# A hybrid decoder trunk on eight cores: the attention mask moves from a matmul to a minimum on VectorE, and the expert loops get three overflow weight buffers

## The reference, cut to what matters

```
layer 0:  h += ShortConv(RMSNorm(h));            h += MoE(RMSNorm(h))
          k, v = split(RMSNorm(h) @ W_kv), rotary on k
layer 1:  h += SlidingWindowAttention(RMSNorm(h)); h += MoE(RMSNorm(h))
out = RMSNorm(h)

attention: blocks of 128 queries; the keys are those of the block before and of the block itself
  diff = qi - kj + BLOCK
  band = (diff >= 0) & (diff < WINDOW)          # WINDOW = BLOCK = 128
  s = where(valid, s, -1e30);  p = softmax(concat([s, sink]))[..., :-1];  o = p @ v
MoE: 4 groups of 8 experts; every token takes the top 2 experts of its top group
  out += (silu(t @ w_gate[e]) * (t @ w_up[e]) * combine[:, e]) @ w_down[e]
```

## Time and profile before

| | before |
|---|---|
| median of 3 runs | 1888.91 us (1885.78 to 1893.54) |
| the profiled execution | 1888.96 us, span of its slowest core 1887.9 us |
| spans of the 8 cores | 1857.4 to 1887.9 us |
| PE busy | 1374.8 us (73%) |
| DVE, ACT, POOL busy | 784.3, 806.6, 556.0 us |
| the 16 DMA engines | 325.18 MB moved, 172 GB/s on average |
| HBM | 574.05 MB read, 171.44 MB written |

### The profile page before, as it was taken

One profiled execution on the slowest core, in us unless ns is written; L12 is line 12 of the kernel. 1 busy time (PEld: TensorE's weight loads), 2 busy tenths in 40 slices (PEclk: granted clock), 3 DMA queues, 4 the chain that ended last, 5 costly groups with the idle time before them and its releaser, 6 DMA issues.

```text
span 1887.9 us, 34378 instructions; the slowest of 8 cores (1857.4 to 1887.9 us)
## 1 busy us (share of the span) xinstructions
PE 1374.8 (73%) x11371; PEld 969.8 (51%) x11467; DVE 784.3 (42%) x2116; ACT 806.6 (43%) x1592; POOL 556.0 (29%) x596
## 2 busy tenths in 40 slices
PE   3899299953487586773589888889853688788744
PEld 2787277732366465652335444454332566666533
DVE  2667177763122132221334555555452223232267
ACT  2454155431133233332476667566631234343354
POOL 4001111215132232322544333423214333232270
PEclk8999699976788798886788889889875899898965
DMA  9999987953989789687999545753683698889687
GB/s 166 263 222 113 129 116 110 161 112 110 201 208 218 192 212 238 151 216 176 168 144 152 114 86 105 137 90 73 91 156 123 167 263 213 273 225 278 181 282 253
DMA packets 104966, 325.18 MB, mean 172 GB/s; under 512 B 35009, under 2 KB 45633, under 8 KB 95960
## 3 DMA queue, kind: packets, MB, share of 16 engines
q0 software_dynamic: 63968, 191.22, 57.1%
q1 hardware_dynamic: 40824, 131.75, 20.1%
HBM read 574.05 MB, written 171.44 MB: 395 GB/s over the span
## 4 chain that ended last, share of the span: by engine, by line
PE 44%; DMA 30%; DVE 8%; issue 8%; ACT 7%; POOL 2%; DVEq 0%; ACTq 0%; another core or an unknown queue 0%; POOLq 0%; SPq 0%
PE psb L906 10%; DMA sb_wov<-wcat,sb_o_rw 8%; DMA sb_arena<-wcat 7%; PE psb L445 6%; DMA xs<-sb_xr,sb_slot 5%; PE psb L925 5%; DMA sb_arena<-wcat,sb_o_rw 4%; PE psb L1203 4%; PE psb L1260 3%; PE psb L614 3%; DMA sb_arena<-w_in 2%; PE psb L496 2%; PE psb L868 2%; PE psb L1298 2%; PE psb L1263 2%
## 5 line engine op out<-in xcount | busy, mean ns | idle before, releaser
L913 DVE TENSOR_TENSOR sb_hd<-psb,sb_sil 128x256 bf16<-128x256 f32 (+1 forms) x128 | 58.6, 458 | 515.3 <-PE psb L906 481.6
L906 PE MATMUL psb<-sb_xT,sb_arena 128*128 128x160 bf16 x2048 | 185.9, 260 | 77.3 <-DMA sb_arena<-wcat 76.1
L906 PEld LDWEIGHTS psb<-sb_xT,sb_arena 128*128 128x128 bf16 x2048 | 172.7, 110 | 103.9 <-issue 103.0
L445 PE MATMUL psb<-sb_xnA,sb_arena 128*128 128x256 bf16 (+1 forms) x1728 | 199.7, 275 | 16.2 <-DMA sb_arena<-w_in 11.7
L445 PEld LDWEIGHTS psb<-sb_xnA,sb_arena 128*128 128x128 bf16 x1728 | 166.6, 102 | 40.5 <-issue 21.4
L925 PE MATMUL psb<-sb_arena,sb_hd 128*32 128x512 bf16 (+1 forms) x600 | 157.3, 390 | 2.5 <-issue 0.8
L162 POOL DMA_INDIRECT xs<-sb_xr,sb_slot x66 | 68.3, 1035 | 263.2 <-DVE sb_cv L464 108.5
L933 ACT ACTIVATE sb_yh<-psb 32x1024 f32<-32x1024 f32 x64 | 64.8, 1013 | 182.6 <-PE psb L925 182.6
L911 ACT ACTIVATE sb_sil<-psb 128x256 f32<-128x256 f32 (+1 forms) x128 | 52.8, 412 | 209.2 <-PE psb L906 208.5
L875 ACT ACTIVATE sb_xT<-psb 128x1024 bf16<-128x1024 bf16 (+1 forms) x96 | 76.1, 810 | 127.7 <-PE psb L868 76.0
L1287 DVE TENSOR_TENSOR sb_OT<-psb,sb_rden 64x256 bf16<-64x256 f32 x128 | 53.3, 417 | 172.4 <-ACT sb_rden L1284 99.6
(11 more groups left out here) (187 smaller groups left out, 2750.8 us busy)
## 6 DMA issues: line engine op xcount, KB each, us to landing
wst<-wcat POOLq DMA_DIRECT2D x76, 768.0 KB, 18.8
sb_arena<-wst SPq DMA_DIRECT2D x38, 1536.0 KB, 15.4
sb_arena<-wcat POOLq DMA_DIRECT2D x26, 1536.0 KB, 15.1
ys<-sb_ym SPq DMA_DIRECT2D x64, 512.0 KB, 10.5
sb_xg<-xs SPq DMA_DIRECT2D x64, 256.0 KB, 8.2
xs<-sb_zrow POOLq DMA_DIRECT2D x1, 10240.0 KB, 95.7
sb_h<-xT POOLq DMA_DIRECT2D x8, 1024.0 KB, 63.7
ys<-sb_yh SPq DMA_DIRECT2D x64, 128.0 KB, 9.9
```

What stands on the lines that cost most here:

```text
L445: tr.op("pe", lambda e: e.matmul(ph(bank, half, n), lhsT=wcol(j, c, part), rhs=xn[p2][:, c, :n], start=(c == 0), stop=(c == NCH - 1)), rea ...
L906: tr.op("pe", lambda e: e.matmul(ps[:, bank * 512 + f * n:bank * 512 + (f + 1) * n], lhsT=w_[:, col:col + 128], rhs=x_[:, c, 0:n], start=( ...
```

## The change

**Mask.** The mask matmul is gone: the second score matmul closes the bank. After the exponential, DVE takes, in place, the minimum of `PT` and a table that holds 3e38 where a key may be seen and 0 elsewhere. It is one `tensor_tensor` of 128 x 1024 in bf16 for a unit, with the table broadcast over the 4 query heads. It stands in `SC`, behind the exponential.

**Expert loops.** A third buffer for overflow weights; `load_wo` of block j + 3 follows block j. The list `held` is gone: every main expert's load goes out in `DN` of the expert three before. The first overflow step follows main expert 3 and not 2. To make room, `xo` has four buffers for five, `xh` one for two, and the two `yh` tiles lie in one, on partitions 0 to 31 and 32 to 63.

```diff
@@ phase_moe
-                NW, NXO, NXT = 3, 5, 5
+                NW, NXO, NXT, NWO = 3, 4, 5, 3
-                wo1 = sb(st_, "wov", [128, 6144], BF16)
-                wo = [wo1[:, :], arena[:, 3, :]]
+                wo1 = [sb(st_, "wov%d" % i, [128, 6144], BF16) for i in range(2)]
+                wo = [wo1[0][:, :], arena[:, 3, :], wo1[1][:, :]]
-                for i in range(2):
+                for i in range(NWO):
                     tr.op("pool", lambda e: e.memset(wo[i], 0.0), writes=woB[i])
-                    xh = [sb(s2, "xh%d" % i, [128, D], BF16) for i in range(2)]
+                    xh = [sb(s2, "xh", [128, D], BF16)]
-                    yh = [sb(s2, "yh%d" % i, [T2, D], F32) for i in range(2)]
+                    yh_ = sb(s2, "yh", [2 * T2, D], F32)
+                    yh = [yh_[T2 * i:T2 * i + T2, :] for i in range(2)]
@@ the list of steps
-                        want = -(-(e - 1) * J // (NE - 2)) if e > 1 else 0
+                        want = -(-(e - 2) * J // (NE - 3)) if e > 2 else 0
@@ DN
                             if i + NW < NE:
-                                if (i + NW) in STAGED[l]:
-                                    load_w(l, i + NW)
-                                else:
-                                    held.append(i + NW)
+                                load_w(l, i + NW)
                         else:
...
-                            if i + 2 < J:
-                                load_wo(i + 2)
-                            while held:
-                                load_w(l, held.pop(0))
+                            if i + NWO < J:
+                                load_wo(i + NWO)
@@ the loop
-                    for j in range(2):
+                    for j in range(NWO):
                         load_xo(j)
                         load_wo(j)
...
                         DN(k)
-                        if k == 2 or seq[k] == ("m", NE - 1):
-                            while held:
-                                load_w(l, held.pop(0))
@@ SC
-                                                           start=(K_ is KA), stop=False),
-                                  reads=[KB_[r][k_]] + QB_[q][k_], writes=[PB[kbi]], sig=False)
-                        tr.op("pe", lambda e: e.matmul(o, lhsT=identb[:], stop=True, start=False,
-                                                       rhs=mask[:, kbi * 128:kbi * 128 + 128].unsqueeze(1).to_broadcast([128, 4, 128])),
-                              reads=[tabB, cB], writes=[PB[kbi]])
+                                                           start=(K_ is KA), stop=(K_ is KB)),
+                                  reads=[KB_[r][k_]] + QB_[q][k_], writes=[PB[kbi]], sig=(K_ is KB))
                     tr.op("act", lambda e: e.activation(out=PT[ui % 2][:], in_=ps[:, 0:1024], func=AF.Exp, scale=0.125),
                           reads=[PB[0], PB[1]], writes=[PTB[ui % 2]])
+                    pt = PT[ui % 2][:, :].rearrange("p (k i x) -> p k i x", k=2, i=4)
+                    tr.op("dve", lambda e: e.tensor_tensor(out=pt, in0=pt, in1=mask[:, :].rearrange("p (k x) -> p k x", k=2).unsqueeze(2)
+                                                           .to_broadcast([128, 2, 4, 128]), op=ALU.min),
+                          reads=[tabB], writes=[PTB[ui % 2]])
@@ prep_shared
-    S["mask"] = f(np.concatenate([np.where(k > q, 0.0, -30000.0), np.where(k <= q, 0.0, -30000.0)], axis=1))
+    S["mask"] = f(np.concatenate([np.where(k > q, 3e38, 0.0), np.where(k <= q, 3e38, 0.0)], axis=1))
```

More of the change, by code:

```diff
@@ L810, in phase_moe @@
                     xgB = [Buf("xg%d" % i) for i in range(3)]
-                    xh = [sb(s2, "xh%d" % i, [128, D], BF16) for i in range(2)]
-                    xhB = [Buf("xh%d" % i) for i in range(2)]
+                    xh = [sb(s2, "xh", [128, D], BF16)]
+                    xhB = [Buf("xh")]
                     xT = [sb(s2, "xT%d" % i, [128, NCH, CAP], BF16) for i in range(NXT)]
@@ L831, in load_x @@
                         if e % 4 == 0:
-                            g, q = e // 4, (e // 4) % 2
+                            g, q = e // 4, 0
                             tr.dma("sp", "xh%d" % q, [(xh[q][:].bitcast(U16), xs[4096 + g * 128:4096 + (g + 1) * 128, :], xsB, [xhB[q]])])
@@ L840, in load_wo @@
                     def load_wo(j):
-                        p = j % 2
+                        p = j % NWO
                         tr.idma("wo%d" % p, [(wo[p], O["rw"][:, ovcol[j]:ovcol[j] + 1], wcat_d[l][:], False, NE * 128 - 1, [O["B"]], woB[p])])
@@ L860, in of @@
                             return i, CAP, w[i % NW], wB[i % NW], xT[i % NXT], xTB[i % NXT]
-                        return i, 128, wo[i % 2], woB[i % 2], xU[i % 3], xUB[i % 3]
+                        return i, 128, wo[i % NWO], woB[i % NWO], xU[i % 3], xUB[i % 3]
                     def turn(src, sB):
@@ L888, in XT @@
                             g = i // 4
-                            b, pv = turn(xh[g % 2], xhB[g % 2])
+                            b, pv = turn(xh[0], xhB[0])
                             for r in range(4):
@@ L932, in DN @@
                             tr.op("dve", lambda e: e.tensor_copy(out=ym[p][:], in_=y2(4, 128)), reads=[PB[4], PB[5]], writes=[ymB[p]])
-                            tr.op("act", lambda e: e.activation(out=yh[p][:], in_=y2(6, T2), func=AF.Copy),
+                            tr.op("act", lambda e: e.activation(out=yh[p], in_=y2(6, T2), func=AF.Copy),
                                   reads=[PB[6], PB[7]], writes=[yhB[p]])
                             tr.dma("sp", "ym%d" % p, [(ys[i * 128:(i + 1) * 128, :], ym[p][:].bitcast(I32), [ymB[p]], [ynew()])])
-                            tr.dma("sp", "yh%d" % p, [(ys[4096 + i * T2:4096 + (i + 1) * T2, :], yh[p][:].bitcast(I32), [yhB[p]],
+                            tr.dma("sp", "yh%d" % p, [(ys[4096 + i * T2:4096 + (i + 1) * T2, :], yh[p].bitcast(I32), [yhB[p]],
                                                        [ynew()])])
                             if i + NW < NE:
-                                if (i + NW) in STAGED[l]:
-                                    load_w(l, i + NW)
-                                else:
-                                    held.append(i + NW)
+                                load_w(l, i + NW)
                         else:
@@ L958, in phase_moe @@
                     overflow_setup(l, 7)
-                    for j in range(2):
+                    for j in range(NWO):
                         load_xo(j)
                         load_wo(j)
-                    for j in range(2, NXO):
+                    for j in range(NWO, NXO):
                         load_xo(j)
-                    held = []
-                    last_ov = max(j for j in range(J) if j % 2)
+                    last_ov = max(j for j in range(J) if j % NWO == 1)
                     for k in range(K):
```

2 lines of the change are left out of this document (1 added, 1 removed).

## The result

The changed kernel takes 1818.40 us (median of 4 runs, 1814.97 to 1828.48) against 1888.38 for the kernel before in the same session; the ratio is 0.9635, with a 95% interval of 0.9592 to 0.9678. It is 70 us faster, where 99 were forecast.

The account below looks back on a forecast made before the run. It took the expert loops to be set by transfers or their order, the stream stage mostly by PE. Loops 35 + 28, starts 4 + 2 and mask 30 made 99 us: about 1790, range 1750 to 1855 holding 0.8.

Parts of the forecast that it names:

- rival 3: Stream stage: the mask gives nothing, as the minimum is 1.28 us or DVE's order delays rotary products; 1820, chance 0.13.
- The loops go to a share of 0.92: Expert loops: with loads issued early the DMA engines' share rises from 0.84 to 0.92, saving 35 and 28 us.
- Rival 1: Expert loops: already at the DMA engines' pace, so only the mask and the starts gain; 1853, chance 0.14.
- Loads no longer held: Expert loops: loads go out 5.4 us earlier in the second loop, answering PE's stall of 5.0 to 5.9.
- The leads, 2.5 and 1.5 pairs: Expert loops: main loads now get 2.5 pairs (19 us); gathers had 1.5 (12 us) before and get 2.5 afterwards.
- Waits for `arena<-wcat` nearly gone: Expert loops, a sign that the forecast holds: PE's waits for these weights nearly vanish, with DMA share 0.9 or more.
- much over 15 us: Expert loops, a sign that the prediction is wrong: the converting loads take much over 15 us each.
- Rival 2: POOL's queue, GU of an overflow step: gathers stuck behind early loads make the kernel slower, 1993; chance 0.03.
- The starts of the stages, 6 us: First overflow step, now fifth of the list: most of PE's `xo` wait goes, 4 us in layer 0, 2 in layer 1.
- The extra clear of a weight buffer: Stage start: costs POOL 5.22 us, inside its 7.11 us wait for indices before the first gather, so nothing.
- The mask, 30 us: Stream stage: PE gets 38 us from dropped mask matmuls, DVE's minimum of 0.7 us falls in a gap; 30 saved.
- I leave a fifth of it to new small waits: Stream stage: of PE's 38 us a fifth is lost since ACT and DVE share the plan; 30 saved, from 0 to 40.

Follow-up runs that it names:

- old order: The changed kernel with the first overflow step behind main expert 2, as before the change: 1806.30 us, ratio 0.9551 to the kernel before.
- the run with less ACT work: The changed kernel without ACT's 8 scalings for k and v in the tiles behind the second: 1815.19 us, ratio not settled.
- 27 copied: The changed kernel with 27 instead of 22 experts of layer 1 copied to bf16 in the stream stage: 1797.79 us, ratio 0.9495.

## Why the prediction was right or wrong, point by point

**Direction and range.** 1790 forecast, 1818 measured: faster, inside the range of 1750 to 1855, outside the narrower 1765 to 1815. The time came out near rival 3's 1820, but not by its mechanism: the mask gave half, not nothing.

**The loops go to a share of 0.92.** Right in size, though 0.92 was a choice between 0.84 and 0.99: 363 and 290 us forecast for the windows of core 0, 352 and 288 measured, at shares of 0.94 and 0.93 with unchanged engine work. Rival 1, that the loops were at the engines' pace already, is out; the engines had 0.84, not their limit.

**Why the share rises.** Here the step was wrong, and that 63 us forecast and 66 measured for the loops agree owes something to luck. "Loads no longer held" was to do it, and the third buffer was there to keep the gathers from being late. The runs make a table of the two, sums of both expert stages in us:

| | list kept | loads at once |
|---|---|---|
| two buffers | 767.1 | 791.3 (new order) |
| three buffers | 724.0 | 695.5 |

All but the marked one are in the old order. The third buffer alone takes off 43. Without it the early loads cost 24, of which up to 7 may belong to the new order; its profiled execution was also 6 us over the mean of its eight. With the buffer they take off another 28. The timeline of one cycle that I had read was of the second loop, where main loads stall; in the first loop 70 of the 108 us of waits were for gathers, and the sum never used that. The stall of 11.36 in the earlier trace rows came where two overflow steps follow each other: PE was there 2.1 us after the gather's issue.

**The leads, 2.5 and 1.5 pairs.** Wrong by half a pair each. In the earlier trace rows the slot is free at 1558.53 and PE comes for it at 1578.95 - 5.03 = 1573.92: 15.4 us, two pairs, and not 19. For a gather it is one pair with two buffers, and two with three. So the spare time that the prediction saw behind a load of 15 us was not there, and once the loads took 19.1 us PE still had to wait for them. "Waits for `arena<-wcat` nearly gone" did not come, and the converting loads taking "much over 15 us" was one of its own signs of being wrong.

**Gathers stuck behind early loads.** Rival 2's mechanism is real and decides with two buffers. The run with them lost 15 us against before, with stalls of 6.4 us on average and 14.9 at most. With a third buffer the lead, two pairs, was enough for most: 4 waits of at most 4.8 us in the first loop of core 0.

**The starts of the stages, 6 us.** Wrong. PE's wait of 4.57 us for `xo` went, but the step that took its place is main expert 3, whose load had only just been issued. I priced the wait that goes and did not ask what is late next. In layer 0 it cost 7 us; 4 gained were forecast.

**The extra clear of a weight buffer, at nothing.** Right as far as it shows: POOL still waited 3.94 us for the indices before its first gather, where it was 7.11 before.

**The mask, 30 us.** The mechanism was right and the size off by a factor of two. PE got its 37 us, against 38 forecast. The minimum takes 0.69 us against 0.7, and mostly lies beside other work, but not as free as forecast: it costs 2.5 to 9 us, and PE waited for it 13 times, 11.8 us in all, which was another of the signs of being wrong. The step that failed is the last: "I leave a fifth of it to new small waits". It was more than half. Of what is taken from PE 0.4 arrives, 0.5 to 0.6 without the minimum, and of what is then taken from ACT 0.7; so ACT's work stands on the path, and that its chain was nearly as long as PE's is the explanation that fits, not one that was measured. The earlier trace rows had ACT at 39.6 of 58 us, and I compared DVE with PE there and not ACT.

The Trainium skill's 690 ns for the minimum, from "VectorE: DVE Perf Modes", is what the trace shows where nothing is in the way, 692 at the median. What I had not taken into account stands in "SBUF — State Buffer", in the list on the shared port pair: an operation of DVE with two inputs in SBUF and one of POOL that reads SBUF exclude each other for a whole instruction. The trace agrees, with the ten minimums that ended 0.55 or 0.56 us behind an operation of POOL.

**The sum.** 99 forecast. By the means over the cores of the profiled executions 79 were gained: 66 in the expert stages (63 + 6 forecast), 15 in the stream stage (30), and 2.5 lost in the stages that were not touched. The slowest core shows 70, because core 0 was 18 us over the mean in the first expert stage before, and core 3 is 11 over it in the second now.

What stays open: why only single cores have such a longer expert stage, and why that of the run with less ACT work came out 7.7 us longer on average than that of a kernel with the same loop.

## What to carry to other kernels

When transfers of two kinds share one queue, give the small ones enough buffers before you let the large ones out earlier: here early loads cost 24 us with two buffers (part of it by the new order) and gained 28 with three. Count the steps between a buffer's release and its next use in a trace. For a loop near its transfers' pace, take engine share times length as the work, see that it stays the same, and move work to a stage with room until that stage's share is used up. Before you price what a busy engine gives up, look for the second-longest chain, through every engine, and for an edit of the order of steps ask which load now comes due first.

## What the runs showed of the hardware that was not expected

A `tensor_tensor` of 128 x 1024 bf16 on DVE, in place and with a broadcast second input, takes 0.69 us, but up to 3.21 us when it meets an operation of POOL with two float32 inputs in SBUF. Ten of 64 were over 0.8 us, and each of them ended 0.55 or 0.56 us behind the end of POOL's. In two of the ten the minimum had started some 0.5 us ahead of POOL's operation by the record, and waited all the same; the record's times on POOL are rough. In the other direction, two of POOL's 16 products of 128 x 1024 took 2.61 us where the rest took 2.16 to 2.19.

What an indirect transfer of POOL brings, issued 3.9 us behind a converting load of 1.5 MB, was taken up by PE only 13.2 us after its issue; PE had come for it after 6.9. Copying one more expert ahead (a converting read, and a write of 1.5 MB in bf16) adds 13 to 17 us to the engines' work in the stream stage, by the means of the cores: 459 us with 27 copied against 375 in the changed kernel and 392 with the old order. The stage's work is not the same to the microsecond even for the same bytes, as these two show; in the first expert loop it repeated within 2% (336 to 343).
